# Router products and transposes by column block among the output projections

## The chip, the cores and the metric

One Trainium2 chip, one of its cores. The metric is the device time of one execution in microseconds, lower is better. PE is TensorE, DVE VectorE, ACT ScalarE, POOL GpSimd, SP SyncE.

## What is computed

One layer of a trunk over 320 tokens (256 of a prompt, 64 of a sample), model width 1024: a norm, a wide input projection, three branches (mLSTM, gated MLP with a spatial product, attention on a memory), a gated sum of them, an output projection, and behind it a hierarchical mixture of experts. The part that matters here:

```python
mixed = gates[:, :, 0] * br_mlstm + gates[:, :, 1] * br_gmlp + gates[:, :, 2] * br_mem
x = x + mixed @ p["w_out"]
x = x + hier_moe(rmsnorm(x, p["norm_moe_g"]), ...)

def hier_moe(x, ...):                      # 4 groups of 8 experts, 2 of the best group
    p_group = softmax(xf @ w_rg + b_rg)
    p_top, grp = top_k(p_group, 1)
    e_logits = (xf @ w_re + b_re).reshape(-1, N_GROUPS, EXPERTS_PER_GROUP)
    e_in = take_along_axis(e_logits, grp[:, :, None], axis=1)[:, 0]
    top_vals, top_idx = top_k(e_in, 2)
    p_exp = softmax(top_vals) * p_top
    for e in range(32):
        hidden = silu(xf @ w_g[e]) * (xf @ w_u[e])
        y = y + combine[:, e:e + 1] * (hidden @ w_d[e])
```

Everything is float32. The kernel makes each large product from three float32r products (high times high, high times rest, rest times high), so every weight unit is split once into a high part and a rest.

## The kernel before

The tokens are three tiles, of 128, 128 and 64 rows. `make_steps` writes out one list of steps, and every engine walks that list in order and does its own share of each step. A step has a ring of PSUM banks (`pj` for the large projections, `ms` for the rest, four banks each; PE may be four steps ahead in a ring) and an engine that empties its bank (A or D). An engine that waits in one step does nothing of the later ones.

Weights of the dense part come in 64 units of 1 MB (256 columns). SP issues unit n when the split of unit n-2 is done. ACT makes the high part (`unit_first_part`, L871), DVE the rest (`unit_second_part`, L1180), each behind the last step of unit n-2 in its order. The output projection is the last four units: steps `res` (u, i), u a block of 256 columns and i a token tile, 24 products each (L572). DVE adds the result to the residual `x_tm` (L1421). After `res` (1, 0) ACT and DVE also split the first two expert units (L875, L1189), which SP has issued behind the last dense unit; units 2 to 4 follow, unit 5 waits for the end of the gather.

After the last `res` step of each tile comes the norm: ACT squares the row block (L1050) with a sum, DVE makes the variance, ACT the root (L1052), DVE refines the reciprocal root (`refine`, L1152 to L1156) and writes `xs_tm`, the row times the root and the gain (L1433). Then:

- `hnT` (i, half): PE transposes `xs_tm` (L707), DVE and ACT empty the banks into `hnT` (L1437, L1056). ACT makes the high part of the rows for the gather (`hn_high`, L879), DVE the rest (`hn_rest`, L1175).
- `router`: eight products of a 36 column weight with `hnT` (L524); DVE adds the bias (L1446).
- `lgt`: transposed back to token rows (L716); DVE finds the best group and the two best experts (L1452 to L1473).
- `ranks`: products with a triangle of ones give each token its slot in its group (L722, L721, L724). DVE makes the keys (L1475), the one-hots `og` (L1169), the number of levels (L1477 to L1482), and then the weights of the two experts (`pone_r`, to L1502).
- `gather`: 16 groups of three products bring the token rows of each group together (L742), ACT copies them to `xg` (L1074). `slot_weights` (L752) brings the weights to the slots. Then, for each of 32 experts, `gate_up` (L777), Silu on ACT (L1079), the product with the slot weight on DVE (L1510), `down` (L799), and a `scatter` per group (L813). One expert reads 3 MB of weights in three units through six places.

The gain vectors `gm_g` and `nf_g` are loaded by ACT (L1037) before `res` (0, 0), the router weights by POOL near the start (L1629, L1630).

## Time and profile before

| | us |
|---|---|
| median of 3 runs (lowest, highest) | 935.36 (933.21, 936.63) |
| the profiled execution | 934.54 |
| its span | 932.7 |
| PE busy | 870.5 (93%) |
| DVE busy | 602.2 (65%) |
| ACT busy | 482.1 (52%) |
| mean granted clock of PE | 0.981 |

The page gives the busy time of each engine, its share in 40 equal slices of 23.3 us, the chain of waits that ended last, and the costliest groups of instructions. The chain is 65% PE, 11% DVE, 11% DMA, 8% ACT. Lines are those of the kernel before.

### The profile page before, as it was taken

How to read it: one execution, taken by the hardware profiler on the slowest of the kernel's cores; microseconds unless marked ns; L12 is line 12 of the kernel's file. 1: busy time of each engine (PE TensorE's matmuls, PEld its weight loads, DVE VectorE, ACT ScalarE, POOL GpSimd, SP SyncE). 2: the span in 40 equal slices, each digit the busy share in tenths (PEclk: the TensorE clock that was granted, in tenths of full speed). 3: DMA queues.
4: the chain of work that ended last, by engine and by line, in shares of the span. 5: the costliest groups of instructions: out<-in, count | busy, mean ns of one | idle time of the engine just before them, and what ended most of it. 6: DMA issues, size and time to landing. Idle time of an engine off the chain costs nothing.

```text
span 932.7 us, 13074 instructions
## 1 busy us (share of the span) xinstructions
PE 870.5 (93%) x5259; PEld 779.7 (84%) x5259; DVE 602.2 (65%) x803; ACT 482.1 (52%) x602; POOL 47.6 (5%) x109
## 2 busy tenths in 40 slices
PE   4999999989999999899999999599999999999992
PEld 4889988879989989899999999278777887787871
DVE  4564467762344356386555555747888989898874
ACT  4564466653333235354334334557777767667652
POOL 6002011110011011000000000000000000000000
PEclk9999999989999999999999999799999999999997
DMA  9547343333446857745444465029999999999951
GB/s 277 174 137 253 122 144 102 102 104 102 136 81 111 149 110 120 177 137 161 145 131 137 161 219 189 0 83 345 347 356 354 349 354 346 347 347 345 347 181 59
DMA packets 99234, 182.91 MB, mean 196 GB/s; under 512 B 5384, under 2 KB 71168, under 8 KB 99168
## 3 DMA queue, kind: packets, MB, share of 16 engines
q1 hardware_dynamic: 95264, 171.47, 57.9%
q0 software_dynamic: 3104, 8.37, 3.3%
q10 hardware_dynamic: 800, 2.18, 1.0%
q8 instruction: 44, 0.72, 0.3%
q14 instruction: 22, 0.18, 0.1%
HBM read 176.17 MB, written 5.82 MB: 195 GB/s over the span
## 4 chain that ended last, share of the span: by engine, by line
PE 65%; DVE 11%; DMA 11%; ACT 8%; issue 4%; SPq 0%; DVEq 0%; ACTq 0%
PE pj L524 32%; PE pj L777 14%; PE pj L799 8%; DMA arena<-in_w_in 4%; ACT unit_r L871 3%; DVE unit_r L1180 3%; DMA arena<-in_w_exp_down 3%; DMA arena<-in_w_exp_up 2%; DMA arena<-in_w_mem_k 1%; ACT w_r L875 1%; DVE w_r L1189 1%; PE ms L646 1%; PE ms L813 1%; PE ms L742 1%; PE ms L524 1%
## 5 line engine op out<-in xcount | busy, mean ns | idle before, releaser
L1180 DVE TENSOR_TENSOR unit_r<-arena,unit_r 128x2048 fp32r<-128x2048 f32 x64 | 146.7, 2291 | 210.6 <-ACT unit_r L871 210.5
L1189 DVE TENSOR_TENSOR w_r<-arena,w_r 128x2048 fp32r<-128x2048 f32 x96 | 219.4, 2289 | 47.3 <-ACT w_r L875 46.2
L524 PE MATMUL pj<-xn_r,unit_r 128*128 128x320 f32 x1536 | 235.3, 311 | 1.2 <-DVE unit_r L1180 1.2
L524 PEld LDWEIGHTS pj<-xn_r,unit_r 128*128 128x128 f32 x1536 | 225.6, 188 | 7.4 <-issue 3.3
L875 ACT ACTIVATE w_r<-arena 128x2048 fp32r<-128x2048 f32 x96 | 183.9, 1917 | 54.0 <-DMA arena<-in_w_exp_up 36.3
L777 PE MATMUL pj<-w_r,xg 128*128 128x512 f32 x768 | 191.0, 398 | 0.0
L777 PEld LDWEIGHTS pj<-w_r,xg 128*128 128x128 f32 x768 | 141.9, 189 | 30.6
L871 ACT ACTIVATE unit_r<-arena 128x2048 fp32r<-128x2048 f32 x64 | 122.2, 1909 | 48.8 <-DMA arena<-in_w_in 23.0
L799 PE MATMUL pj<-w_r,hidT 128*128 128x512 f32 x384 | 93.1, 391 | 2.8 <-DVE w_r L1189 1.6
L799 PEld LDWEIGHTS pj<-w_r,hidT 128*128 128x128 f32 x384 | 71.7, 188 | 19.9 <-DVE w_r L1189 3.4
L524 PE MATMUL pj<-unit_r,xn_r 128*128 128x256 f32 (+1 forms) x576 | 70.0, 282 | 2.5 <-DVE unit_r L1180 2.5
L524 PEld LDWEIGHTS pj<-unit_r,xn_r 128*128 128x128 f32 (+1 forms) x576 | 68.2, 172 | 3.0 <-issue 3.0
L524 PE MATMUL pj<-br_r,unit_r 128*128 128x320 f32 x384 | 59.7, 311 | 1.6 <-issue 1.6
L524 PEld LDWEIGHTS pj<-br_r,unit_r 128*128 128x128 f32 x384 | 56.7, 188 | 3.0 <-issue 2.9
L524 PE MATMUL pj<-unit_r,mn_r 128*128 128x256 f32 x384 | 50.1, 291 | 9.4 <-DVE mn_r L1184 7.2
L524 PEld LDWEIGHTS pj<-unit_r,mn_r 128*128 128x128 f32 x384 | 48.4, 198 | 10.2 <-issue 9.6
L572 PE MATMUL pj<-unit_r,mix_r 128*128 128x256 f32 (+1 forms) x288 | 34.3, 281 | 0.5 <-DVE arena L1421 0.5
L572 PEld LDWEIGHTS pj<-unit_r,mix_r 128*128 128x128 f32 (+1 forms) x288 | 34.0, 170 | 0.7 <-DVE arena L1421 0.7
L1085 ACT ACTIVATE hidT<-ms 128x256 fp32r<-128x256 f32 x32 | 12.3, 384 | 34.1 <-PE ms L787 34.1
L524 PE MATMUL pj<-u_r,unit_r 128*128 128x320 f32 x192 | 28.8, 309 | 0.0
L524 PEld LDWEIGHTS pj<-u_r,unit_r 128*128 128x128 f32 x192 | 28.3, 188 | 0.0
L1196 DVE SCALAR_TENSOR_TENSOR arena<-arena,prT 128x323 f32<-128x323 f32 x48 | 26.7, 556 | 1.7
(322 smaller groups left out, 741.5 us busy)
## 6 DMA issues: line engine op xcount, KB each, us to landing
arena<-in_w_in SPq DMA_DIRECT2D x40, 1024.0 KB, 5.2
arena<-in_w_exp_gate SPq DMA_DIRECT2D x64, 512.0 KB, 4.6
arena<-in_w_exp_up SPq DMA_DIRECT2D x64, 512.0 KB, 6.1
arena<-in_w_exp_down SPq DMA_DIRECT2D x64, 512.0 KB, 5.4
arena<-in_w_mem_k SPq DMA_DIRECT2D x4, 1024.0 KB, 11.5
arena<-in_w_mem_v SPq DMA_DIRECT2D x4, 1024.0 KB, 5.2
arena<-in_w_br_mem SPq DMA_DIRECT2D x4, 1024.0 KB, 10.0
arena<-in_w_br_mlstm SPq DMA_DIRECT2D x4, 1024.0 KB, 5.2
```

The source lines that it names most:

```text
L524: last = mm(bank_of(s)[0:out_rows, 0:out_cols], l, r, start=k == 0, stop=k == len(pairs) - 1)
L572: last = mm(b[0:n, 0:256], mix_r[:, p, k, t0:t0 + n], w[:, q, k, :], start=k + m == 0, stop=k == KC - 1 and m == 2)
L646: last = mm(b[:, dk * n:dk * n + n], v, pT[:, h % 2, j, t0:t0 + n], start=j == 0, stop=j == 1)
L742: last = mm(gather_banks[q % 4], hn_r[:, part, i, c, :], og[:, i, :, :].rearrange("p g s -> p (g s)"), start=i == 0, stop=i == 2)
L777: last = mm(pj[:, x % 2, :].rearrange("p (h n) -> p h n", h=2), xg[:, k0 + k, xp, g * SLOTS:(g + 1) * SLOTS], w[:, wp, k, :, :], start=k0 ...
L799: last = mm(pj[:, 2 + half, :], hidT[:, x % 2, xp, c, :], w_r[u % NS][:, wp, c * D + half * 512:c * D + half * 512 + 512], start=e == 0 an ...
L871: af(unit_r[n % RING][:, 0, :], ringw[:, n % RING, :], ACT.Copy).then_inc(u_hi, 1)
L875: af(w_r[u % NS][:, 0, :], raw_w[u % NS], ACT.Copy).then_inc(m_hi, 1)
L1085: af(hidT[:, x % 2, 0, :, :].rearrange("p a b -> p (a b)"), ms[:, x % 2, 0:DE], ACT.Copy).then_inc(m_hth, 1)
L1180: v.tensor_tensor(unit_r[n % RING][:, 1, :], ringw[:, n % RING, :], unit_r[n % RING][:, 0, :], ALU.subtract).then_inc(u_lo, 1)
L1189: v.tensor_tensor(w_r[u % NS][:, 1, :], raw_w[u % NS], w_r[u % NS][:, 0, :], ALU.subtract).then_inc(m_lo, 1)
L1196: ins = v.scalar_tensor_tensor(o, r[:, j:j + CONVW], prT[:, P_CW + 16 * j + c:P_CW + 16 * j + c + 1], o, ALU.mult, ALU.add)
```

## The change

The norm is taken apart. Its gain goes on at once, block by block: after each `res` (u, i) DVE writes `xs_tm` = `x_tm` times the gain for those 256 columns. Its reciprocal root `rs` goes on later: on the router logits (one scaled add for each tile, in token rows), on the argument of Silu (a scale from a column), and into the slot weights (`pw` times `rs`; each group's slot weights get two more columns that hold `rs`, 10 for 8). The sum of squares is collected in 12 pieces. So transposes and router products no longer need the whole row:

- `hnT` is now by column block c (three transposes, one bank), in a ring `hx` of three `ms` banks, and `logits` c is one router product that adds into the fourth bank. Blocks 0 to 5 stand between the `res` steps of u = 1, 2, 3; blocks 6 and 7 behind them. ACT empties the even blocks, DVE the odd ones.
- The router weights are padded to 128 columns, and POOL clears and loads them at `gate` (1, 7). The bias is loaded to all partitions.
- `hn_high` and `hn_rest` are done in two pieces, columns 0 to 95 of 128 at `res` (3, 0) on ACT and at u = 3 and in `ranks` on DVE, the last quarter behind the norm. The high parts and the rests lie in two places, POOL clears their unused rows. The gather does its eight high parts first, then the rests.
- In `ranks` the level count comes behind the one-hots and the rests, and frees the bank early.
- ACT loads the two gain vectors at `br` (1, 0). Expert units 4 and 5 swap places; unit 4 is issued when the last `res` product is done.

```diff
@@ make_steps
         for i in range(3):
             step("res", u, i, ring="pj", eng="D", unit=n, last=i == 2)
+            if u and i < 2:
+                for c in (2 * u - 2, 2 * u - 1):
+                    if i == 0:
+                        step("hnT", c, ring="hx", eng="AD"[c % 2])
+                    else:
+                        step("logits", c, ring=None, eng=None)
+    step("hnT", 6, ring="hx", eng="A")
+    step("hnT", 7, ring="hx", eng="D")
     step("moe_norm", ring=None, eng=None)
-    for i in range(3):
-        for half in range(2):
-            step("hnT", i, half, eng="DA"[half])
-    step("router")
-    step("lgt")
-    step("ranks")
+    step("logits", 6, ring=None, eng=None)
+    step("logits", 7, ring=None, eng=None)
+    step("lgt", ring="hx")
+    step("ranks", ring="hx")
@@ sync, load_unit
                     elif u == 4:
-                        sp.wait_ge(u_lo, len(UNITS))
+                        sp.wait_ge(ready["pj"], NPJ)
@@ tensor
+                if kind == "logits":
+                    c, = a
+                    if c == 0:
+                        pe.wait_ge(s_par3, 16 * 4)
+                    pe.wait_ge(*done("hnT", c))
+                    last = mm(ms[:, 3, 0:T], wr[:, c, :], hnT[:, c, :], start=c == 0, stop=c == KC - 1)
+                    if c == KC - 1:
+                        last.then_inc(s_logits, 1)
...
+                    c, = a
+                    for i, (t0, n) in enumerate(TILES):
+                        pe.wait_ge(s_xs, 3 + 3 * (c // 2) + i + 1)
+                        last = tr(b[:, t0:t0 + n], xs_tm[0:n, i, c * 128:(c + 1) * 128], ident[0:n, 0:n])
@@ tensor, gather
+                pe.wait_ge(s_hnh, 3 * lv + 6)
                 for q in range(NQ):
-                    c, part = q // 2, q % 2
+                    c, part = q % KC, q // KC
+                    if q == KC:
+                        pe.wait_ge(s_hnl, 3 * lv + 6)
@@ scalar
+                    if c == 0:
+                        act.wait_ge(*done("br", 0, 7))
+                        act.wait_ge(*done("sp", 7))
+                        act.dma_start(gm_g, I["norm_moe_g"][0, :].partition_broadcast(128)).then_inc(s_gm, 16)
+                        act.dma_start(nf_g, I["norm_final_g"].partition_broadcast(128)).then_inc(s_nfg, 16)
...
-                elif kind == "res" and a == (1, 0):
-                    unit_high(0, 0)
-                    unit_high(0, 1)
...
+                elif kind == "res":
+                    u, i = a
+                    k = 3 * u + i
...
+                    act.wait_ge(*done("res", u, i))
+                    act.wait_ge(s_ss, 5 + k)
+                    af(junk[0:n, :], x_tm[0:n, i, u * 256:(u + 1) * 256], ACT.Square, accum_out=sq[0:n, i, u:u + 1]).then_inc(s_ss, 1)
+                    if a == (1, 0):
+                        unit_high(0, 0)
+                        unit_high(0, 1)
+                    elif a == (3, 0):
+                        act.wait_ge(ready["pj"], _by_name["res", 2, 2]["at"] + 1)
+                        act.wait_ge(s_xs, 3 + 9)
+                        for j in range(3):
+                            hn_high(j, 0, 96)
+                elif kind == "hnT" and a[0] % 2 == 0:
+                    c, = a
+                    af(hnT[:, c, :], b[:, 0:T], ACT.Copy).then_inc(free, 1)
+                elif kind == "moe_norm":
+                    act.wait_ge(s_var, 5)
+                    af(sd[:, 20:23], var[:, 20:23], ACT.Sqrt).then_inc(s_sd, 1)
+                    act.wait_ge(s_xs, 3 + 12)
+                    for i in range(3):
+                        hn_high(i, 96, 128)
                     unit_high(0, 2)
                     unit_high(0, 3)
@@ vector
+                    dve.wait_ge(*done("res", u, i))
+                    cs = slice(u * 256, u * 256 + 256)
+                    v.tensor_tensor(xs_tm[0:n, i, cs], x_tm[0:n, i, cs], gm_g[0:n, cs], ALU.mult).then_inc(s_xs, 1)
                     if (u, i) == (1, 0):
                         unit_rest(0, 0)
                         unit_rest(0, 1)
...
+                    if u == 3 and i < 2:
+                        hn_rest(i, 0, 96, i + 1)
+                elif kind == "hnT" and a[0] % 2:
+                    c, = a
+                    v.tensor_copy(hnT[:, c, :], b[:, 0:T]).then_inc(free, 1)
...
+                elif kind == "moe_norm":
+                    dve.wait_ge(s_ss, 5 + 12)
+                    link(v.tensor_reduce(ssx[:, 20:23], sq[:, :, :], axis=AX.X, op=ALU.add))
+                    v.tensor_scalar(var[:, 20:23], ssx[:, 20:23], 1.0 / D, EPS, ALU.mult, ALU.add).then_inc(s_var, 1)
+                    refine(5, 20, 23)
+                elif kind == "logits" and a[0] == KC - 1:
+                    dve.wait_ge(s_logits, 1)
+                    v.tensor_copy(lgT, ms[:, 3, 0:T]).then_inc(s_lgT, 1)
@@ vector, ranks
+                    link(v.tensor_reduce(cnt[:, 0:1], b[0:1, 3 * G:4 * G], axis=AX.X, op=ALU.max))
+                    v.tensor_copy(cnt[:, 3:4], cnt[:, 0:1]).then_inc(free, 1)
                     token_onehots()
-                    link(v.tensor_reduce(cnt[:, 0:1], b[0:1, 3 * G:4 * G], axis=AX.X, op=ALU.max))
+                    hn_rest(2, 0, 96, 3)
+                    for i in range(3):
+                        hn_rest(i, 96, 128, 4 + i)
@@ gpsimd
+                elif kind == "gate" and a == (1, 7):
+                    pool.wait_ge(*done("gate", 1, 7))
+                    g.memset(wr, 0.0).then_inc(s_wrz, 1)
+                    pool.wait_ge(s_wrz, 1)
+                    pool.dma_start(wr[:, :, 0:G], ...).then_inc(s_par3, 16)
+                    pool.dma_start(wr[:, :, G:G + E], ...).then_inc(s_par3, 16)
```

## Rows read from the trace of the kernel before

**Rows 1.** The page: PE's busy share in 40 slices, in tenths.
```profile
PE   4999999989999999899999999599999999999992
```

**Rows 2.** Windows: stretch, length; busy us of PE, PEld, DVE, ACT, POOL; granted clock; DMA share; GB/s.
```profile
590.00:620.00 30.00, 22.64 (x89) 15.27 (x89) 21.71 (x62) 17.27 (x22) 0.00 (x0) 0.77 0.00 1
700.00:800.00 100.00, 98.41 (x436) 79.14 (x435) 90.41 (x66) 71.77 (x60) 0.00 (x0) 1.00 0.99 350
```

**Rows 3.** Timeline, the output projections: start, length, engine, line, operation, count, idle before.
```profile
546.65 22.84 PE L572 MATMUL pj<-unit_r,mix_r 128*128 128x256 f32 x192
552.42 0.74 DVE L1421 TENSOR_TENSOR arena<-arena,pj 128x256 f32<-128x256 f32 x2
...
557.38 2.29 DVE L1180 TENSOR_TENSOR unit_r<-arena,unit_r 128x2048 fp32r<-128x2048 f32 x1 [1.62 <-ACT unit_r L871]
...
561.89 1.92 ACT L875 ACTIVATE w_r<-arena 128x2048 fp32r<-128x2048 f32 x1 [4.55 <-DMA arena<-in_w_exp_up]
...
565.38 1.92 ACT L875 ACTIVATE w_r<-arena 128x2048 fp32r<-128x2048 f32 x1 [1.57 <-DMA arena<-in_w_exp_up]
...
567.33 2.29 DVE L1189 TENSOR_TENSOR w_r<-arena,w_r 128x2048 fp32r<-128x2048 f32 x1 [1.19 <-ACT w_r L875]
...
570.00 11.50 PE L572 MATMUL pj<-unit_r,mix_r 128*64 128x256 f32 x96 [0.51 <-DVE arena L1421]
```

**Rows 4.** Single lines (ns least/median/most), and from the timeline eight transposes.
```profile
L987 ACT ACTIVATE junk<-arena x12: 416/417/419, 263.0 to 358.3; 128x256 f32<-128x256 f32 x8, 64x256 f32<-64x256 f32 x4
L987 ACT ACTIVATION_READ_ACCUMULATOR junk<-arena x12: 186/186/188, 263.4 to 358.6; 128x1 f32 x8, 64x1 f32 x4
L998 ACT ACTIVATE arena<-pj x24: 414/438/439, 288.2 to 539.8; 128x320 f32<-128x320 f32 x24
L879 ACT ACTIVATE hn_r<-arena x3: 2036/2047/2059, 586.8 to 591.4; 128x1024 fp32r<-128x1024 f32 x2, 64x1024 fp32r<-64x1024 f32 x1
L1175 DVE TENSOR_TENSOR hn_r<-arena,hn_r x3: 1989/1991/2002, 592.9 to 596.7; 128x1024 fp32r<-128x1024 f32 x2, 64x1024 fp32r<-64x1024 f32 x1
581.34 1.04 PE L707 MATMUL ms<-ident,arena 128*128 128x128 f32 x8
```

**Rows 5.** Windows of 1 us about two changes of the granted clock (columns as in rows 2).
```profile
587.00:588.00 1.00, 0.00 (x0) 0.00 (x0) 0.93 (x3) 1.00 (x1) 0.00 (x0) 0.50 0.00 0
...
596.00:597.00 1.00, 1.00 (x3) 0.37 (x2) 1.00 (x2) 1.00 (x1) 0.00 (x0) 0.50 0.00 0
597.00:598.00 1.00, 1.00 (x5) 0.41 (x4) 1.00 (x1) 0.98 (x2) 0.00 (x0) 0.97 0.00 0
```

**Rows 6.** The chain that ended last, from the norm to the gather: start, length, what.
```profile
577.54 0.17 DVE var L1429
...
578.93 1.28 DVE arena L1433
...
591.86 7.06 PE ms L524 x16
...
597.83 1.09 PE ms L524 x4
...
599.01 0.55 DVE arena L1446
...
600.42 0.18 DVE arena L1452
...
604.55 1.89 DVE og L1169 x3
...
607.42 2.90 PE ms L742 x6
...
611.94 1.40 PE ms L742 x6
```

**Rows 7.** The same chain near the start, and a window there (columns of rows 2).
```profile
15.10 12.56 DMA arena<-in_w_mem_k
...
23.00:24.00 1.00, 1.00 (x11) 1.00 (x10) 0.00 (x0) 0.00 (x0) 0.00 (x0) 1.00 1.18 208
```

More of the change, by code:

```diff
@@ L323, in build_kernel @@
         off[0] = B0 + 2 * KC * G * SLOTS + 3 * G * SLOTS
-        pone_r = rounded("pone_r", off[0], 2, 3, E)
-        take(2, 3, E)
+        pone_r = rounded("pone_r", off[0], 2, 3, G * GW)
+        take(2, 3, G * GW)
+        weights = take(3, G * GW)
         one = [take(3, E) for _ in range(2)]
@@ L504, in _ @@
                 load_unit(0, u)
-            sp.wait_ge(*done("ranks"))
+            sp.wait_ge(s_more, 1)
             need = sp.value_load(more[0:1, 0:1], min_val=0, max_val=LEVELS - 1)
@@ L741, in gather @@
                     for i in range(3):
-                        last = mm(gather_banks[q % 4], hn_r[:, part, i, c, :], og[:, i, :, :].rearrange("p g s -> p (g s)"), start=i == 0, stop=i == 2)
+                        last = mm(gather_banks[q % 4], hn_r[part][:, i, c, :], og[:, i, :, :].rearrange("p g s -> p (g s)"), start=i == 0, stop=i == 2)
                     last.then_inc(m_gather, 1)
@@ L751, in slot_weights @@
                         for i in range(3):
-                            last = mm(ms[:, 0, g * EPG:(g + 1) * EPG], og[:, i, g, :], pone_r[:, part, i, g * EPG:(g + 1) * EPG],
+                            cs = slice(g * GW, (g + 1) * GW)
+                            last = mm(ms[:, 0, cs], og[:, i, g, :], pone_r[:, part, i, cs],
                                       start=g + part + i == 0, stop=part + i == 3, skip_group_check=True)
@@ L1051, in _ @@
-                    act.wait_ge(s_var, 5 + i)
-                    af(sd[:, 20 + i:21 + i], var[:, 20 + i:21 + i], ACT.Sqrt).then_inc(s_sd, 1)
-                elif kind == "hnT" and a[1] == 1:
-                    i = a[0]
-                    t0, n = TILES[i]
-                    af(hnT[:, 4:8, t0:t0 + n], b.rearrange("p (a t) -> p a t", t=128)[:, :, 0:n], ACT.Copy).then_inc(free, 1)
-                    if i == 0:
-                        act.wait_ge(ready["pj"], NPJ)
-                    hn_high(i)
-                elif kind == "router":
+                    act.wait_ge(*done("res", u, i))
@@ L1078, in silu_gate @@
                 until(act, m_hid, E * lv + x - 1)
-                af(sgh[:, x % 2, :], pj[:, x % 2, 0:DE], ACT.Silu).then_inc(m_silu, 1)
+                if x == 0:
+                    act.wait_ge(m_combined, lv + 1)
+                af(sgh[:, x % 2, :], pj[:, x % 2, 0:DE], ACT.Silu, scale=comb[:, x // EPG, EPG:EPG + 1]).then_inc(m_silu, 1)
             def hidden_high(lv, x):
@@ L1556, in _ @@
             level(0)
-            dve.wait_ge(*done("ranks"))
+            dve.wait_ge(s_more, 1)
             need = dve.value_load(more[0:1, 0:1], min_val=0, max_val=LEVELS - 1)
@@ L1563, in _ @@
                     v.tensor_scalar(key, key, -float(SLOTS), None, ALU.add).then_inc(t_key, 1)
[L1564 removed]
+                    for part in hn_r:
+                        v.memset(part[64:128, 2, :, :].bitcast(FP32), 0.0)
                     dve.wait_ge(t_key, lv)
```

164 lines of the change are left out of this document (76 added, 88 removed).

## Prediction

> **What bounds the kernel now.** I read the slices of the page first, to find where TensorE (PE) is not full. After the start there is one such place, the 26th slice of 40 [rows 1]. The windows then give the sizes: 22.6 us of PE work in the 30 us from 590 to 620, at a granted clock of 0.77, and 98.4 in the 100 from 700 to 800, where the DMA engines are at 0.99 as well [rows 2]. So the kernel is bound by PE nearly throughout, by PE and weight transfers together in the expert stage, and between the two lies a bridge: the last output projection ends at 570.00 + 11.50 = 581.5 us, the first gather product starts at 607.42 [rows 3, 6]. Those 25.9 us are a chain of norm, transposes, router, logits, ranks and one-hots. It is what the change shortens. Behind the gather everything hangs on its end: the weights of expert unit 5 are issued when the gather is done, and PE starts on the experts after the slot weights. A shift of the gather is therefore a shift of the end, one for one.
>
> The third view is the order of time in the stretch in front, the twelve output projection steps `res` (u,i). They start at 546.65 and eight of them run without a gap in 22.84 us, 2.855 us each; then PE waits 0.5 us, to 570.00 [rows 3]. The wait is short only because PE can be four banks ahead: ScalarE (ACT) waits for expert unit 0 until 561.89 and for unit 1 until 565.38, VectorE (DVE) splits unit 1 until 567.33 + 2.29 = 569.62, and neither serves PE in between [rows 3]. This decides the case.
>
> **The change part by part.** All instants are on the time axis of the profiled execution.
>
> Added to PE among the projections: for six of eight column blocks three transposes and a router product. Eight transposes take 1.04 us, so three are 0.35 with pipelining; a product of 320 columns is two passes, and four passes take 1.09 us, so 0.54 [rows 4, 6]. (a) 6 x 0.89 = **+5.3**.
>
> The wait that takes the place of the old one. PE's order is now res(1,0), hnT 0, hnT 1, res(1,1), logits 0, logits 1, res(1,2). res(1,0) ends at 546.65 + 4 x 2.855 = 558.1, the transposes at 558.8, res(1,1) at 561.6. logits 0 wants ACT's copy of hnT 0, and ACT has that behind both of its expert units: 565.38 + 1.92 = 567.3, and a copy of 320 columns is 0.44 [rows 3, 4], so 567.75. logits 1 wants DVE's copy, behind the split of unit 1: 569.62 + 0.5 = 570.1. PE has the 0.54 us of logits 0 to do in 561.6 to 570.1, so it idles 8.0 us, against 0.5 before. (b) **+7.5**. Queued behind it is every later projection; nothing of the change brings the expert units sooner. The two gain vectors (1 MB) go out earlier now, but SyncE issues the expert units behind the last dense unit, on a split that has not moved.
>
> The clock. PE's last projection ended at 581.5, and with little to do after it the engine stood at 0.50 in the window from 587; the router products started at 591.86, and the clock came back at 597.0, 5.1 us later. The gather shows the same: 2.90 us for its first six products, 1.40 for six later ones [rows 5, 6]. A hole of 6.2 us (561.6 to 567.8) with little in the 2 us after it should cost the same drop from 2.4 to 1.2 GHz; at half speed for 3 to 5 us after 570.1 PE loses half of that. (c) **+2.0**, bounds 0 and 4.
> The Trainium skill, page "TensorE: Matmul & The Clock Gate", section "HAM oscillation — how this bites in real kernels", speaks against a change like this one: a wait for a transfer in the middle of a stream of products puts the array back to the lower clock, and the next stretch begins cold. The trace agrees with it [rows 5]; without the rule the forecast would be 2.0 us lower.
>
> Later projections. With res(1,2) ending at 575.5, the split of the last w_out unit comes after it: ACT 576.7 to 578.6 behind a square, DVE to 581.0 (2.29 each as at 557.38 [rows 3]). DVE then adds res(2,0), ACT squares (0.42 + 0.19 [rows 4]) and copies hnT 2 by 582.5; PE is there at 581.9. (d) **+0.6**. The split itself is in time. At res(3,0), which ends at 589.3, ACT has three `hn_high` of 96 of 128 columns before its copy of hnT 4: DVE's add to 589.9, square to 590.5, 3 x 2.05 x 0.75 = 4.6 us [rows 4], copy, 595.6. PE has finished hnT 4, 5 and res(3,1) at 592.9 and waits for logits 4. (e) **+2.8**, bounds 0 (copies as fast as plain ones, 1.06 us for 1024) and 3.5. DVE's own `hn_rest` pieces (1.99 x 0.75 [rows 4]) fit beside that.
> Sum in the projections: 5.3 + 7.5 + 2.0 + 0.6 + 2.8 = 18.2; they end at 599.7 instead of 581.5.
>
> The bridge. Before: from 581.5 to the copy of the group logits at 600.42 [rows 6], 18.9 us. After: DVE add and gain product 2 x 0.41 plus hand-over (two adds take 0.74 [rows 3]) to 600.8; hnT 6 and 7 to 601.5; DVE copies hnT 7 to 602.15; logits 7 is done at 602.9, but DVE is then in the norm: sum of squares 0.2, then variance, root and refinement 578.93 - 577.54 = 1.39 [rows 6], to 603.8. The logits copy 0.5 (0.55 [rows 6]), transposes 0.5, three scaled adds 0.4: 605.3. That is 5.6 us, **-13.3**. The norm's reciprocal root is off the front of the chain but still in it, since the logits copy is queued behind it on DVE. From there to the gather: 600.42 to 604.55 as before, then a reduction and a copy (0.36), the one-hots 1.89 and the hand-over, 6.45 against 607.42 - 600.42 = 7.0, because the level count is out of it [rows 6]. **-0.55**. The rests of the last pieces (3.0 us on DVE) come after the one-hots; the first eight gather groups need only the high parts and take over 5 us, so they are covered. ACT's last pieces and the two expert units end by 608.5, before the gather. The gather again begins at the lower clock, PE having idled as before: 0. The wider slot weights (40 for 32 columns, 24 products) and Silu's scale from a column: 0, covered by PE's expert products; uncovered it would be some 0.1 us. POOL's clears run beside ACT and DVE: 0, at most 0.5.
>
> The start. The router weights leave POOL's early queue. There the chain runs over the transfer of a w_mem_k unit, 15.10 to 27.66, and at 23 us the engines carry only 208 GB/s at a full share [rows 7]. 144 KB at 350 GB/s are 0.4 us; two such poor windows would be 1.5. I take **-0.6**.
> The Trainium skill, "DMA: Bandwidth & Descriptors", section "Why small descriptors are slow (HBM only)", says each packet has a fixed cost besides its bytes; the 16-byte pieces would then be worth more than 0.4, up to the 1.5. The trace shows the poor windows but not whose they are. At the new place (about 542) the same pieces meet the w_out unit loaded there, which ACT wants only at 556.4: 0.
>
> Sum: 18.2 - 13.3 - 0.55 - 0.6 = **+3.75 us**. The profiled execution took 934.54 us (932.7 of it its span), so 938.3; the median of the runs is 935.36, so **939.1**, said as 939.0. About 0.5%, 4.7 us, is what a measurement of this kernel can tell from no change; 930.7 and 940.0 are its bounds.
>
> **Rivals.**
> R1, the hole is not there: PE finds the copies ready, because units 0 and 1 land by 558 or the copies are not behind them. Then (b) and (c) fall, 9.5 us: 929.6. For it: the gain vectors no longer go out in front of them. Against: their issue waits for the same split as before, and what lands last of the two was looked at by ACT at 565.38 [rows 3], seven microseconds too late.
> R2, the slower side: the wait for logits 4 in (e) drops the clock a second time. Then res(3,2), the last transposes and products run at 1.2 GHz: up to 2.9 + 1.2 us more, 942 to 943.5. It decides from the point where that wait lasts as long as the hole from 581.5 to 587 [rows 5]; 2.8 us speaks against it. A first drop that lasts through res(2,0) gives the same 2 to 3 us.
> R3, the shift is smaller by 3 to 4 us: the start gives 1.5 and (e) shrinks to near nothing since DVE and ACT catch up. 935 to 936.5.
> R4, the change does not do what it says: the router products stay behind the norm. Then nothing is gained of the 13.3: some 7 us of it (products, copies) is lost again, 946. Against: `logits` waits for its hnT copy alone.
>
> **How the numbers follow.** Forecast (937 to 942, with (c) 0 to 3): 0.58. R1 0.14; R2 0.15; R3 0.11; R4 0.02. Faster by over 0.5%: R1 without its weak end, 0.13. Slower: R2, R4 and some 0.37 of the forecast's own spread, 0.39. Same: 0.48. The range from 932.0 to 943.5 leaves out R1 and R4 and little more.
>
> **What would show it.** Right: PE idle about 6 us near 562 with ACT's copy of hnT 0 as releaser and 1.4 us near 569 with DVE's; a granted clock of 0.5 near 567 to 573; a wait of 2 to 3 us before logits 4; the last projection at 599 to 600; the gather's start at about 612 against 607.4; the expert stage unchanged in length. Wrong: a PE that is full from 546 to the last projection, or an expert stage that changes its length.

## The result and the profile after

The changed kernel takes 939.28 us (median of 8 runs, 938.4 to 944.59), the kernel before beside it on the same chip 934.35 (8 runs, 932.24 to 937.59): a ratio of 1.0057, 95% interval 1.0031 to 1.0083. That is 4.9 us more where 3.75 were forecast. On another chip the two stand at 935.64 and 930.27, ratio 1.0053 (1.002 to 1.0087). The profiled execution of the changed kernel took 939.52 us, its span is 937.6.

PE's slices on the page: the soft place of [rows 1], the 26th slice with five tenths, has become two, the 24th with eight (539 to 563 us, the new hole) and the 26th with six.
```profile
PE   4999999989999999999999989699999999999993
```
The windows that answer to [rows 2] (busy us of PE, PEld, DVE, ACT, POOL; granted clock; DMA share; GB/s): the stretch of the bridge holds the same PE work, and the expert stage is still PE and transfers at once.
```profile
590.00:620.00 30.00, 22.50 (x101) 17.99 (x102) 21.28 (x80) 16.28 (x28) 0.00 (x0) 0.83 0.10 36
700.00:800.00 100.00, 97.49 (x431) 78.02 (x430) 88.21 (x65) 72.03 (x59) 0.00 (x0) 1.00 0.97 344
```
The timeline of PE through the projections, which answers to [rows 3] (start, length, line, operation, count, idle before and who ended it). L595 is `res`, L729 `hnT`, L552 `logits`:
```profile
555.04 3.12 PE L595 MATMUL pj<-unit_r,mix_r 128*128 128x256 f32 x24
563.42 1.41 PE L552 MATMUL ms<-arena 128*128 128x320 f32 x2 [5.26 <-ACT arena L1084]
565.73 1.44 PE L552 MATMUL ms<-arena 128*128 128x320 f32 x2 [0.91 <-DVE arena L1468]
566.50 7.04 PE L595 MATMUL pj<-unit_r,mix_r 128*64 128x256 f32 x48
573.38 1.15 PE L729 MATMUL ms<-ident,arena 128*128 128x128 f32 x6
574.46 3.12 PE L595 MATMUL pj<-unit_r,mix_r 128*128 128x256 f32 x24
577.41 1.24 PE L552 MATMUL ms<-arena 128*128 128x320 f32 x4
578.25 6.05 PE L595 MATMUL pj<-unit_r,mix_r 128*64 128x256 f32 x48
584.14 1.15 PE L729 MATMUL ms<-ident,arena 128*128 128x128 f32 x6
585.22 3.11 PE L595 MATMUL pj<-unit_r,mix_r 128*128 128x256 f32 x24
590.38 1.34 PE L552 MATMUL ms<-arena 128*128 128x320 f32 x4 [2.05 <-ACT arena L1084]
```
The hole is where it was said to be, between res(1,1) and logits 1, and the wait before logits 4 behind it. ACT's timeline shows what its copies (L1084) stand behind: the two expert units, the second of which waits for its transfer, and later the three `hn_high` (L901).
```profile
557.49 1.91 ACT L897 ACTIVATE w_r<-arena 128x2048 fp32r<-128x2048 f32 x1 [0.21 <-DMA arena<-in_w_exp_up]
561.04 1.91 ACT L897 ACTIVATE w_r<-arena 128x2048 fp32r<-128x2048 f32 x1 [1.64 <-DMA arena<-in_w_exp_up]
562.86 0.42 ACT L1084 ACTIVATE arena<-ms 128x320 f32<-128x320 f32 x1
...
585.21 4.79 ACT L901 ACTIVATE hn_h<-arena 128x768 fp32r<-128x768 f32 x3
589.90 0.42 ACT L1084 ACTIVATE arena<-ms 128x320 f32<-128x320 f32 x1
```
Windows about the hole, columns as in [rows 5]: the clock goes to 0.50 at 561.8, in the hole, and is back at 568.6, 2.1 us into the projections that follow.
```profile
561.00:562.00 1.00, 0.00 (x0) 0.00 (x0) 0.72 (x1) 0.96 (x1) 0.00 (x0) 0.89 1.04 422
562.00:563.00 1.00, 0.00 (x0) 0.00 (x0) 0.01 (x1) 1.00 (x2) 0.00 (x0) 0.50 1.05 426
...
567.00:568.00 1.00, 1.00 (x6) 1.00 (x5) 0.00 (x0) 0.00 (x0) 0.00 (x0) 0.50 0.00 0
568.00:569.00 1.00, 1.00 (x8) 1.00 (x7) 0.00 (x0) 0.00 (x0) 0.00 (x0) 0.70 0.00 0
```

The stages of every profile taken, in us: the start of res(0,0); the projections up to the end of res(3,2); the bridge from there to the copy of the group logits; from that to the first gather product; the gather; and from the first product of expert 0 to the end. (2.6 us of slot weights lie between the last two, in all of them.) Ratios are to the kernel before, with 95% intervals; a dash is a single time.

| kernel | res(0,0) | projections | bridge | to gather | gather | experts | ratio |
|---|---|---|---|---|---|---|---|
| before | 546.65 | 34.85 | 18.92 | 7.00 | 12.73 | 309.96 | |
| before_again | 540.03 | 34.90 | 18.51 | 7.62 | 13.69 | 310.05 | - |
| after | 542.62 | 51.90 | 5.75 | 7.54 | 13.62 | 313.58 | 1.0057 (1.0031 to 1.0083) |
| after_again | 538.44 | 53.00 | 5.75 | 8.32 | 13.70 | 311.39 | 1.0053 (1.002 to 1.0087) |
| units_later | 538.77 | 47.74 | 5.74 | 8.02 | 13.12 | 310.31 | 0.9981 (0.9946 to 1.0017) |
| hn_later | 538.56 | 51.28 | 5.75 | 7.01 | 12.55 | 309.85 | 1.0043 (1.0021 to 1.0065) |
| both_later | 547.99 | 41.83 | 7.34 | 8.34 | 13.42 | 310.39 | 0.9944 (0.9913 to 0.9974) |
| interleave_undone | 538.75 | 39.15 | 12.10 | 8.31 | 12.77 | 310.12 | 0.9941 (0.9912 to 0.997) |
| hole_filled | 541.58 | 54.26 | 5.75 | 7.88 | 13.28 | 307.76 | - |
| early_loads | 541.10 | 54.99 | 5.75 | 7.62 | 13.51 | 310.74 | - |
| high_split | 539.50 | 41.83 | 7.25 | 8.32 | 13.81 | 310.60 | 0.9955 (0.9934 to 0.9975) |
| high_split_filled | 538.76 | 41.83 | 6.84 | 8.14 | 11.20 | 308.34 | 0.9934 (0.9905 to 0.9962) |
| rests_behind | 538.67 | 41.84 | 5.75 | 8.10 | 13.06 | 307.68 | 0.9929 (0.9904 to 0.9954) |
| rests_behind_filled | 539.08 | 41.82 | 5.69 | 6.24 | 12.14 | 309.53 | 0.9895 (0.987 to 0.992) |

The ratio of interleave_undone leaves out one of its ten executions, which took 1237.25 us at a mean granted clock of 0.656, where the nine others took 921.7 to 931.0 us at 0.974 to 0.985; what lowered its clock is not known.

### The profile page after: what moved, and what is told of

It reads as the page before. It is cut to its first block and busy times, and to the rows that moved or that the text cites. A ratio compares the mean times of both kernels' runs of the same rounds, so it can differ in the third digit from the quotient of the medians.

```text
span 937.6 us, 13126 instructions
## 1 busy us (share of the span) xinstructions
PE 876.0 (93%) x5259; PEld 784.7 (84%) x5259; DVE 601.2 (64%) x813; ACT 487.5 (52%) x622; POOL 50.5 (5%) x112
## 5 line engine op out<-in xcount | busy, mean ns | idle before, releaser
L595 PE MATMUL pj<-unit_r,mix_r 128*128 128x256 f32 (+1 forms) x288 | 37.1, 288 | 0.0
L595 PEld LDWEIGHTS pj<-unit_r,mix_r 128*128 128x128 f32 (+1 forms) x288 | 35.3, 173 | 1.1 <-issue 0.5
```

The lines of the kernel that those rows point to most:

```text
L595: last = mm(b[0:n, 0:256], mix_r[:, p, k, t0:t0 + n], w[:, q, k, :], start=k + m == 0, stop=k == KC - 1 and m == 2)
```

## The experiments

**The changed kernel and the kernel before, again.** No edit.

> The changed kernel, unchanged, for a second profile on another day of the queue. Theory (two copies queued behind the expert units on ACT and DVE): ratio to before 1.004 to 1.007; in the trace PE idle 5 to 6 us before logits 0, about 1 us before logits 1 and about 2 us before logits 4, twelve projections plus what stands between them 51 to 52 us long. Rival (the time is made in the expert stage, which was 3.6 us longer in the first profile of after, 313.4 against 309.8 us from the first expert product to the end): the holes are there but the expert stage is again about 3.6 us longer. If its length changes from profile to profile by that much, it is the spread of the weight stream and no part of the change.

> The kernel before without an edit, profiled a second time. Eleven profiles of kernels with the change start res(0,0) between 538.4 and 548.0 us, the one profile of before at 546.65. By stages the change costs 5.3 us in the profile of the changed kernel and 7.3 in the second one (projections, bridge, ranks and gather together), and the runs give 4.9. Theory (the change is worth some 1 to 2 us ahead of res(0,0), the rest of the difference there is the spread of one profile to the next): ACT's third unit waits until 27.5 to 28.0 us, res(0,0) starts at 540 to 545, stages from res(0,0) to the expert units within 0.5 us of the first profile of before, the expert stage 308 to 312 us. Rival (the change gives 4 to 8 us ahead of res(0,0)): the start at 546 or later again. Rival (it gives only the 0.85 us of ACT's third unit): the start at 539 to 540, as the median of the others plus 0.9.

The 4.9 us hold on a second chip (5.4 us there). The projections of after_again are 1 us over the expected 51 to 52, and its expert stage is 311.39 us long, so the 3.6 us by which the first profile's exceeded that of before do not come back. The second profile of before is the more instructive: its projections repeat within 0.05 us, its bridge within 0.4, but ranks and gather take 0.6 and 1.0 us more than in the first, with nothing changed; so the expectation of 0.5 us is missed. PE's lines of it (L724 the last of `ranks`, L742 the gather):
```profile
596.52 1.42 PE L724 MATMUL ms<-arena,ones 128*128 128x4 f32 x6
601.06 2.90 PE L742 MATMUL ms<-og,hn_r 128*128 128x512 f32 x6 [3.12 <-DVE more L1482]
603.75 2.77 PE L742 MATMUL pj<-og,hn_r 128*128 128x512 f32 x6
606.31 1.62 PE L742 MATMUL ms<-og,hn_r 128*128 128x512 f32 x6
```
The six rank products take 1.42 us and the second six gather products 2.77. Where in those two stages the clock is low thus differs from one execution to the next, and the 0.5 and 0.9 us by which the changed kernel's first profile exceeds [rows 6] there can't be put down to the change. The ten profiles with the change and without added products in the bridge have 7.0 to 8.3 us to the gather (7.95 in the mean) and 12.6 to 13.8 for the gather (13.3); two profiles of before, with 7.00 and 7.62, 12.73 and 13.69, are too few to tell whether the first of these is longer. res(0,0) starts at 540.03 here and not at 546.65; eleven of the twelve profiles with the change start it between 538.4 and 542.6, one at 547.99.

**Where the hole comes from.** The splits of expert units 0 and 1 one token tile each later:
```diff
-                    if a == (1, 0):
+                    if a == (2, 1):
                         unit_high(0, 0)
+                    elif a == (2, 2):
                         unit_high(0, 1)
```
(and DVE's `unit_rest` in the same way).

> The changed kernel, but ACT and DVE split expert unit 0 behind res (2, 1) and unit 1 behind res (2, 2), no longer both behind res (1, 0). Nothing is left out. Theory: the hole before logits 0 and 1 (8.0 us, of which 0.5 were there before) and the fallen clock (1.3 us) go, and the time falls by 8 to 9.5 us against after, to 930 us; the wait before logits 4 stays at 2 to 3 us or grows by 1 since the unit splits are nearer to it. Rival 1 (the hole only hides time that the weight transfers would need anyway): PE waits elsewhere for the same transfers and the time stays within 2 us of after. Rival 2 (the added PE work and the bridge decide, not the hole): 937 to 939.

The hole before logits 0 and 1 is gone altogether: PE waits for nothing but logits 4 and the last transposes. 6.2 us of waits and the slower clock are saved in front, yet the projections are only 4.2 and 5.3 us shorter than in the two profiles of the changed kernel, since the wait before logits 4 has grown from 2.05 to 5.05 us and what follows is at half speed:
```profile
572.73 3.11 PE L595 MATMUL pj<-unit_r,mix_r 128*128 128x256 f32 x24
580.89 2.50 PE L552 MATMUL ms<-arena 128*128 128x320 f32 x4 [5.05 <-ACT arena L1085]
582.73 3.78 PE L595 MATMUL pj<-unit_r,mix_r 128*64 128x256 f32 x24
```
What PE waits for are ACT's three pieces:
```profile
575.99 4.53 ACT L901 ACTIVATE hn_h<-arena 128x768 fp32r<-128x768 f32 x3
580.41 0.43 ACT L1085 ACTIVATE arena<-ms 128x320 f32<-128x320 f32 x1
```
Counted from res(0,0), PE has finished res(3,1) 8.6 us earlier than in the changed kernel (37.1 in place of 45.7 us), ACT begins the pieces only 5.4 us earlier (37.2 in place of 42.6). This is the place and the mechanism of R2. The gain, 929.68 us against 935.64 on the same chip, falls short of the expected 8 to 9.5 us by what this wait has grown. The time is that of the kernel before, so the hole accounts for what the change costs over it.

**The wait before logits 4.** ACT's three early pieces behind its copy of hnT 4, DVE's behind hnT 5 and at res(3,1); alone, and together with the edit above:
```diff
-                    elif a == (3, 0):
-                        ...
-                        for j in range(3):
-                            hn_high(j, 0, 96)
...
                     af(hnT[:, c, :], b[:, 0:T], ACT.Copy).then_inc(free, 1)
+                    if c == 4:
+                        ...
+                        for j in range(3):
+                            hn_high(j, 0, 96)
```

> The changed kernel with only the early pieces of the gather's rows moved: ACT's three hn_high behind its copy of hnT 4, DVE's hn_rest(0) behind its copy of hnT 5 and hn_rest(1) at res(3,1). The expert units stay where the change has them, so the hole before logits 0 stays. Theory: the wait before logits 4 (2.05 and 2.25 us in the two profiles of the changed kernel) goes, the holes before logits 0 and 1 stay at 5.3 and 0.9 us; projections 49.7 to 50.9 us in place of 51.9 to 53.0; but ACT's third hn_high is now late in the bridge, which grows from 5.75 to about 7.3 as it did where both were moved; net about -0.7 us, 0 to -2, ratio to before 1.003 to 1.006. Rival (wait 4 is set by the expert units, not by hn_high): the wait stays at 2 us, and the whole is 1.5 us slower than the changed kernel.

> As units_later, and also ACT's three high parts of the rows behind its copy of hnT 4, DVE's rest of tile 0 behind its copy of hnT 5 and that of tile 1 at res (3, 1). Nothing is left out. Theory: both kinds of hole go, 10.5 to 12 us less than after, 927 to 929 us, faster than the kernel before by 0.6 to 0.8%. Rival 1 (the second wait returns in another place, since ACT must still do 4.8 us of high parts before its copy of hnT 6): same as units_later. Rival 2 (expert stage absorbs the gain): no more than 3 us less than after.

Alone: the wait before logits 4 is gone, the hole stays (5.56 and 0.90 us), as expected (2.05 us is what the second profile of the changed kernel has there too, not 2.25). The bridge did not grow, and the projections are 0.4 us over the expected range. The gain of 2 us is half taken back after the hole, where res(1,2) and (2,0) take 8.42 us at the lower clock in place of 7.04 and 7.86; the ratio of 1.0043 can't be told from 1.0053. Together: projections 41.83 us, with 0.62 us as the longest wait in them, and a kernel 0.6% faster than before: 9.4 us less than the changed kernel on the same chip, where 10.5 to 12 were expected. The bridge is 7.34 us in place of 5.75.

**Who lengthens that bridge.** First guess: ACT's third piece stands before its copy of hnT 6. It was moved behind the norm's root.
```diff
-                        for j in range(3):
+                        for j in range(2):
                             hn_high(j, 0, 96)
...
+                    hn_high(2, 0, 96)
                     for i in range(3):
                         hn_high(i, 96, 128)
```

> The expert units' splits behind res(2,1) and (2,2), the early pieces of the gather's rows behind the copies of hnT 4 and 5, as in the kernel with both moved, and ACT's third early piece (tile 2) behind the norm's root. Theory: no wait over 0.7 us before any logits step, projections 41 to 43 us; the 1.6 us by which the bridge grew (7.34 against 5.75) was ACT's copy of hnT 6 behind that third piece, so the bridge is back at 5.8 to 6.2 us. Against the kernel before 6 to 8 us more in the projections, 13 less in the bridge, +1 to +2 in ranks and gather by the clock, -0.85 at the start: 4 to 6 us faster, ratio 0.993 to 0.996. Rival (the bridge grew by DVE's rests or by something else): bridge stays above 7 us and the time equals the 926.2 us of the kernel with both moved, ratio 0.9944.

The guess fell: 7.25 us. DVE's timeline shows the cause. L1210 is `hn_rest`, L1457 the add of res(3,2), which PE had finished at 581.33:
```profile
578.66 1.70 DVE L1210 TENSOR_TENSOR hn_l<-arena,hn_h 128x768 fp32r<-128x768 f32 x1 [1.53 <-ACT hn_h L901]
580.29 0.40 DVE L1457 TENSOR_TENSOR arena<-arena,pj 128x256 f32<-128x256 f32 x1
580.73 0.43 DVE L1462 TENSOR_TENSOR arena<-arena 128x256 f32<-128x256 f32 x1
581.07 1.54 DVE L1210 TENSOR_TENSOR hn_l<-arena,hn_h 128x768 fp32r<-128x768 f32 x1
582.53 0.40 DVE L1457 TENSOR_TENSOR arena<-arena,pj 64x256 f32<-64x256 f32 x1
```
The add comes 1.2 us late, behind the second rest. So that one went behind the one-hots:
```diff
-                    if (u, i) == (3, 1):
-                        hn_rest(1, 0, 96, 2)
...
                     token_onehots()
+                    hn_rest(1, 0, 96, 2)
                     hn_rest(2, 0, 96, 3)
```

> The kernel with the third early piece behind the root, and DVE's hn_rest(1) of 96 columns (1.54 us at res(3,1)) moved behind the one-hots. Theory (the bridge is 7.25 to 7.34 us where the expert units and the pieces were both moved, in place of 5.75, because DVE adds res(3,2) 1.4 us after PE has finished it, being in hn_rest(1)): PE's wait before the last hnT 0.7 us in place of 1.9, bridge 5.7 to 6.1 us, projections 41.8, gather start 1.2 to 1.6 us earlier against res(0,0), the rests still in time for the gather's second half; ratio to before 0.992 to 0.995. Rival (something else of DVE, as hn_rest(0) or the adds before, is late as well): bridge 6.5 to 7.3. Rival (the rest now comes too late for the gather): a wait before the ninth gather group of up to 1.5 us, the gain is lost.

Bridge 5.75 us, PE's wait before the last transposes 0.74 in place of 1.89, no wait in the gather. The ratio is 0.9929; the step from 0.9955 is within the intervals, in the trace it is the 1.5 us. ACT's third piece stays behind the root in this kernel; that alone had changed the bridge from 7.34 to 7.25 us, and whether the last step needs it was not run.

**The clock.** 40 products that no result uses, between res(1,1) and logits 0 of the changed kernel:
```diff
+                        for q in range(40):
+                            mm(ms[:, 2, 0:256], mix_r[:, 0, q % KC, 0:128], unit_r[1][:, 0, 0:256], start=True, stop=True)
```

> The changed kernel with 40 products of 128x256 more that PE does between res(1,1) and logits 0, into a bank nobody reads; they add work (no result uses them) and bring no data sooner. Theory (the wait before logits 0 itself stops PE's later work, and the granted clock falls because PE has nothing to do in it): the start of logits 0 stays at the end of ACT's copy of hnT 0, so the time from res(0,0) to the last res changes only by the clock; granted clock 1.0 from 562 to 573 in place of 0.50 to 568; res(1,2) and res(2,0) 5.7 us in place of 7.0; the stretch of the projections 1.3 to 2 us shorter than the 51.9 and 53.0 us of the two profiles of the changed kernel. Rival (the clock fell for another reason, such as heat or the mix of small products): still 0.50 somewhere in 562 to 568, the stretch unchanged. Rival (40 products at 0.11 us are too many): logits 0 starts behind them, up to 1 us later.

The hole stays where it was, as the theory has it: logits 0 starts at ACT's copy, with 0.99 us of idle time left before it and 1.60 before logits 1. The clock did not do what the theory says:
```profile
561.00:562.00 1.00, 0.86 (x8) 0.65 (x6) 0.17 (x1) 1.00 (x1) 0.00 (x0) 1.00 0.96 393
...
564.00:565.00 1.00, 0.00 (x0) 0.00 (x0) 1.00 (x2) 0.00 (x0) 0.00 (x0) 1.00 0.07 29
...
566.00:567.00 1.00, 1.00 (x8) 1.00 (x7) 0.00 (x0) 0.07 (x1) 0.00 (x0) 0.57 0.00 0
```
It stays at 1.00 until about 566.1 and falls when PE is at work again, to 0.50 until 569.6; res(1,2) and (2,0) take 7.59 us. And in this run logits 4 and res(3,2) are at half speed too (2.50 and 3.92 us), behind the same wait of 2.04 us. So what was put into the hole only shifted the fall, from 561.8, within PE's wait, to 566.1, when PE was at work again; how much would hold the clock is not settled by this, and it is one profile.

Products more in the bridge, of the same kind, on top of the kernel with the third piece behind the root (8, 14 and 18 of them) and of the one with the rests behind the one-hots (8, 17 and 10):
```diff
                 elif kind == "lgt":
+                    fill(8)
                     pe.wait_ge(s_lgT, 1)
...
                 elif kind == "ranks":
+                    fill(17)
                     pe.wait_ge(s_route, 1)
...
+                    fill(10)
                 pe.wait_ge(m_onehot, 3 * lv + 3)
```

> The kernel with the third early piece behind the root, and products more in the bridge that no result uses: 8 ahead of the transposes of the logits, 14 ahead of the ranks, 18 ahead of the gather, 128x256 each. Theory (ranks and the gather's first groups are slow because the granted clock has fallen while PE idles in the bridge): granted clock above 0.9 from the last projection into the gather, gather products in 10 to 12 us in place of 13.6, group logits to gather start 7 us or less in place of 7.5 to 8.3; in all 2 to 4 us less than the same kernel without them, ratio to before 0.989 to 0.993. Rival (the added products stand on the path and take as long as they save): the same time within 1 us. Rival (clock falls all the same, since there is still a part of the bridge without products): gather as long as without, 0 to 1 us slower.

> The same with products more that no result uses: 8 ahead of the transposes of the logits, 17 ahead of the ranks, 10 ahead of the gather (before: 8, 14 and 18, where the clock still fell at 591.9 and the 18 took 3.89 us at half speed and put the gather's start 1.7 us behind its one-hots). Theory: ranks at 1.0; the gather starts 0.3 to 0.8 us after the one-hots; gather stage 11.2 to 12.2 us in place of 13.6; group logits to gather start 6.2 to 7.0 us in place of 8.3; ratio to before 0.988 to 0.992. Rival (fewer products let the clock fall or stay low in the gather): gather 12.7 to 13.7 us, the time as without products within 1 us. Rival (the rests behind the one-hots are late against a gather at full clock, which asks for them 5.6 us after its start): a wait of 1 to 2 us before the ninth group.

In the first, ranks and the whole gather run at full speed (11.20 us against 13.81 without), but the clock had fallen at 591.8, behind the ranks, the 18 products took 3.89 us, nearly all of it at half speed, and held the gather back: to the gather it is 8.14 us where 7 or less were expected, and the ratio of 0.9934 can't be told from the 0.9955 without the products. With fewer there PE reads, of the kernel that is the fastest here:
```profile
588.11 0.39 PE L745 MATMUL ms<-arena,before 128*128 128x4 f32 x2 [0.21 <-DVE arena L1507]
...
589.47 0.81 PE L747 MATMUL ms<-arena,ones 128*128 128x4 f32 x6
591.00 2.04 PE L536 MATMUL pj<-mix_r 128*128 128x256 f32 x10 [0.71 <-DVE cnt L1522]
592.83 2.56 PE L771 MATMUL ms<-og,hn_h 128*128 128x512 f32 x6
595.22 1.55 PE L771 MATMUL pj<-og,hn_h 128*128 128x512 f32 x6
```
The six last rank products take 0.81 us where the profile of before_again has 1.42; to the gather it is 6.24 us, the gather 12.14. The time is 920.69 us against 923.48 without the products on the same chip (ratios 0.9895 and 0.9929, whose intervals just overlap), and against 931.17 for before. It is 1.0% faster than before and some 1.6% faster than the changed kernel. In its profile the clock falls once more, from 608.6 to about 612, so that the first 36 products of the experts take longer than in the kernel with 8, 14 and 18:
```profile
607.57 10.16 PE L807 MATMUL pj<-w_r,xg 128*128 128x512 f32 x36
```
against
```profile
609.36 8.64 PE L807 MATMUL pj<-w_r,xg 128*128 128x512 f32 x36
```
That takes back 1.5 of the 2.8 us which ranks and gather gain here over rests_behind. hn_later, without any added products, has such a fall at the same place, so they need not be its cause.

**Without the interleaving.** All transposes and router products behind the last projection, the rest of the change kept:
```diff
-            if u and i < 2:
-                for c in (2 * u - 2, 2 * u - 1):
-                    ...
-    step("hnT", 6, ring="hx", eng="A")
-    step("hnT", 7, ring="hx", eng="D")
+    for c in range(KC):
+        step("hnT", c, ring="hx", eng="AD"[c % 2])
+        if c >= 2:
+            step("logits", c - 2, ring=None, eng=None)
```

> The changed kernel with one part undone: all eight transposes and router products stand behind the last projection (hnT c, then logits c - 2), everything else, the norm taken apart among it, as in after. Nothing is left out. Theory: the projections are 35 us long again with a hole of 0.5 us, 17 us shorter than in after, and the bridge from the last projection to the group logits grows from 5.9 to 9 to 10.5 us; in sum 12 to 13 us less than after, 926 to 928 us, so that the interleaving as it was placed is what costs and the taking apart of the norm is what gives. Rival (the interleaving gives and the norm's rearrangement costs): slower than after, 942 or more.

0.9941: without its title's part the change makes the kernel faster. The projections cost 4.3 us more, not 17.6, as PE can again be four banks ahead of the expert units; the waits left are 2.54 us for DVE's rest of the last w_out unit and 0.62 for a bank. Expected were 35 us of projections and a bridge of 9 to 10.5; both were missed, and the time is 10.1 us below the changed kernel's in place of 12 to 13. The bridge is 12.1 us, 6.8 shorter than before. The transposes no longer wait for the norm: here they begin as the projections end,
```profile
567.77 10.13 PE L591 MATMUL pj<-unit_r,mix_r 128*128 128x256 f32 x72 [2.54 <-DVE unit_r L1210]
577.74 1.72 PE L725 MATMUL ms<-ident,arena 128*128 128x128 f32 x9
```
while in the kernel before those of the last tile begin 7.8 us behind that end (581.5):
```profile
589.31 1.11 PE L707 MATMUL ms<-ident,arena 64*128 64x64 f32 x8 [3.65 <-DVE arena L1437]
```
Interleaving in the order in which hardly anything waits (rests_behind) gives 3.7 us more by stages (47.6 against 51.3 for projections and bridge together); by the runs, 0.9929 against 0.9941 on two chips, that is not told apart.

**The start.** The router weights loaded early once more, into a tile that nobody reads:
```diff
+            pool.dma_start(wr0[:, :, 0:G], I["w_router_group"][0].rearrange("(k p) n -> p k n", p=128)).then_inc(s_extra, 16)
+            pool.dma_start(wr0[:, :, G:G + E], I["w_router_expert"][0].rearrange("(k p) n -> p k n", p=128)).then_inc(s_extra, 16)
```

> The changed kernel with one more load that nobody uses: the two router weights in their 16-byte and 128-byte pieces on POOL's early queue, where the kernel before had them; the late loads stay. Theory (the start gained because these pieces no longer share the engines with the unit of w_mem_k that ACT waits for): ACT's third unit waits until 27.6 to 27.7 us as before, in place of 26.6 to 26.9 us in all seven profiles of the change's kind; that is 0.8 to 1.1 us given back; everything from res(0,0) on as in the changed kernel. Rival (the start gained by the changed issue times of another queue, or by nothing of the change): ACT waits until 26.6 to 26.9 us here too. Rival (dearer than bounded, each piece has a fixed cost): over 28.2 us.

ACT's third unit starts at 28.56 us, later than the 27.6 to 27.7 expected and in the range of the second rival (over 28.2). It starts at 27.68 and 28.01 in the two profiles of before, and at 26.5 to 27.4, 26.84 in the mean, in the eleven with the change and without these loads. With the two loads, and in the changed kernel:
```profile
28.56 1.91 ACT L895 ACTIVATE unit_r<-arena 128x2048 fp32r<-128x2048 f32 x1 [3.85 <-DMA arena<-in_w_mem_k]
```
```profile
26.82 1.92 ACT L893 ACTIVATE unit_r<-arena 128x2048 fp32r<-128x2048 f32 x1 [1.29 <-DMA arena<-in_w_mem_k]
```
The window that answers to [rows 7] in the changed kernel:
```profile
23.00:24.00 1.00, 1.00 (x10) 1.00 (x10) 0.00 (x0) 0.00 (x0) 0.00 (x0) 1.00 1.16 303
```
and with the two loads put back:
```profile
23.00:24.00 1.00, 1.00 (x10) 1.00 (x10) 0.00 (x0) 0.00 (x0) 0.00 (x0) 1.00 1.25 219
```
With these loads the window carries 208 and 256 GB/s in the profiles of before and 219 here; without them 288 to 310 in ten profiles and 195 in one, that of hole_filled. The next window, 24 to 25 us, has no exception: 168, 157 and 129 GB/s with them, 327 to 358 in the eleven profiles without. So the poor stretch is theirs, though a single poor window can come without them. They cost ACT's third unit 1.0 us by the means, 1.7 by this single run; at res(0,0), which starts at 541.10 us here, this is lost in the spread of 538.4 to 547.99.

## Why the prediction was right, point by point

The time is right within its spread (4.9 us for 3.75). For the terms I take the mean of the two profiles of the changed kernel less that of the two of before; together they give +5.35 us. So each measured term has the spread of four executions in it.

| term | forecast | measured |
|---|---|---|
| (a) work among the projections | +5.3 | +7.0 |
| (b) the hole before logits 0 and 1 | +7.5 | +6.8 |
| (c) the clock behind it | +2.0 | +1.8 |
| (d) hnT 2 | +0.6 | 0 |
| (e) the wait for logits 4 | +2.8 | +2.05 |
| the bridge | -13.3 | -13.0 |
| to the gather | -0.55 | +0.6 |
| the gather | 0 | +0.45 |
| before res(0,0) | -0.6 | -2.8 |
| experts | 0 | +2.5 |

- What bounds the kernel: right. The hole stands behind ACT's copy and that behind the expert units; with the units later it is gone (units_later), and the time is that of before.
- (a) was sized too small. The transposes begin 1.08 us before the projection that follows (573.38 to 574.46), the products 0.84 before theirs (577.41 to 578.25): 5.9 us for three such pairs, logits 4 at its 0.94 us, where I had 5.3: a block's transposes cost 0.54 for my 0.35, a product 0.42 for my 0.54. The projections themselves, cut into pieces, take 1.1 us longer, which I left out of the sum: behind each insertion the next steps take 2.95 (res(2,1)), 5.89 (res(2,2) and (3,0)) and 3.04 us (res(3,2)) from start to start, where [rows 3] have 2.855 for one. The kernels without waits agree: 41.84 less the 34.35 us of work of before and a wait of 0.63 is 6.9.
- (b): from the end of res(1,1) at 558.16 to logits 1 at 565.73 are 7.57 us, less 0.42 of work and the 0.5 of [rows 3] 6.65 (6.9 the second time). Of the 7.57 PE idles 6.17 us (6.44 the second time), 5.7 more than before; the rest is logits 0, which takes 1.4 us at the lower clock here and 0.81 at the higher one in hole_filled. The releasers are those forecast. PE comes to it 0.6 us later behind res(0,0) than I had it, so part of (a) is hidden here.
- (c): 1.35 and 2.15 us, within 0 to 4. The page "TensorE: Matmul & The Clock Gate" of the Trainium skill, section "HAM oscillation — how this bites in real kernels", has the next stretch cold after such a wait; the trace agrees, 0.50 from 562 to 568.
- (d) did not occur: it is a wait before logits 2, and neither profile has one. ACT's copy of hnT 2 is done 6.3 us behind the end of res(1,2) (570.7) where I had 7.0, and PE comes to logits 2 6.7 us behind it where I had 6.4.
- (e): the wait is there, on the same releaser, 2.05 us in both profiles. ACT's three pieces took 4.79 us for 4.6; the wait is shorter because PE has finished res(3,1) 4.2 us behind res(3,0), where I had 3.6.
- The bridge: 5.75 us for 5.6. The refinement ends and the logits copy starts on DVE as worked out, one behind the other.
- To the gather: the level count is out of it, as said: the og step starts 5.3 us behind the group logits and PE 2.24 us behind that, where [rows 6] have 2.87. What hides it is the clock in the rank products, the last six of which take 1.42 us in both profiles of the changed kernel and 0.94 in the first of before; at full clock, with the added products, the step takes 6.24 us (rests_behind_filled), for the 6.45 of the forecast. I read one profile's clock there as that of the kernel.
- Before res(0,0): 1.0 us of it, as far as ACT's third unit shows it, is the router weights, more than the 0.6 and within the bound of 1.5. The Trainium skill, "DMA: Bandwidth & Descriptors", section "Why small descriptors are slow (HBM only)", has a fixed cost for each packet; the trace agrees so far that 144 KB cost more than their bytes. The rest of the 2.8 is mainly one profile of before that reached this point at 546.65 where the other did at 540.03.
- Experts: 307.7 to 313.6 us in the twelve profiles with the change, which all have the same code there, 310.02 in their mean, and 310.0 in both profiles of before. So the 2.5 us are the spread of two executions and the forecast's 0 holds, though the prediction called an expert stage of another length a sign of being wrong. In the sum these 2.5 us cancel the term above; that the total came out so close is in part luck of these two.
- R1 is out. R2's second drop is real but its condition was wrong: behind a wait of 2.05 us it is absent in both profiles of the changed kernel and present in early_loads (logits 4 2.30 us, res(3,2) 4.14) and hole_filled, with the same wait. So it does not begin only where the wait is as long as the 5.5 us of [rows 5], and it makes part of the spread of the runs. R3 gave 0.4 us of its start and 0.75 of (e). R4 is out: logits 0 to 5 stand among the projections.

## What to carry to other kernels

Work put into a full stream of products brings along the queues of the engines that empty its banks: before placing a step, list what stands ahead of its copy on each of them, waits for transfers above all, since the slack of the banks (here four of them) is lost the moment PE waits for a copy at once. When one such wait is removed, look for the next in the same queue before timing anything; here three moves were needed, of the expert units, the high parts and a rest, each of which exposed the next, from 1.0057 to 0.9929 (a fourth, of ACT's third piece, did not shorten the bridge). And take a second profile of the kernel before, so that terms under one microsecond are not read from the clock of one execution.

## What the runs showed of the hardware

- The granted clock need not fall within the wait. With 40 products in the hole it fell at about 566.1, when PE had been at work again since 565.26; in the bridge of before_again it fell within the rank products, at 596.2, in that of the first profile at their end, near 604. Identical code has its gather at 12.73 and 13.69 us.
- In hn_later and rests_behind_filled, two of the twelve profiles with the change, the clock falls a second time among the first products of the experts (at 619 and 608.6), with PE busy without a break since the slot weights; 36 products then take 10.2 us for 8.6.
- Behind the same wait of 2.05 us before logits 4 the clock fell in two profiles of four (hole_filled and early_loads, not after and after_again).
- With 144 KB in pieces of 16 and 128 bytes on a queue beside it, the engines carry 129 to 168 GB/s from 24 to 25 us in place of 327 to 358, and a 1 MB unit lands 1.0 us later in the mean.
- The stretch up to res(0,0) ends between 538.4 and 542.6 us in twelve of the fourteen profiles, at 546.65 and 547.99 in two, one of each kind of kernel. Between 380 and 400 ACT waits 8.0 us for a unit of w_in in the first profile of before and not at all in the second; no more was looked at.
